# Preparing the recurrence inside the long convolution: paired low-rank products, key norms by Ln and Exp, key factors on ScalarE, keys on GpSimd

## The chip, the cores and the metric

One core of one Trainium2 chip runs the whole program in one launch. The metric is the device time of that launch in microseconds (us), lower is better; several executions are timed and their median is given. One more execution is taken with the hardware profiler, and every time in the sections on the trace is from it, counted from the start of its span.

## The reference

The model has two layers over 256 context tokens and 256 latent tokens of width 1024. Each layer is a feed-forward half step, a token mixer and a second feed-forward half step, each closed by a residual with LayerNorm. The mixer of the first layer, where the change lies, projects the tokens once and feeds two branches: a long convolution of order 2 (done by a discrete Fourier transform as matrix products), and a bidirectional RWKV-7 recurrence. What the recurrence needs is prepared like this:

```python
kk = heads(k * k_k)
kk = kk / jnp.maximum(jnp.sqrt(jnp.sum(kk * kk, -1, keepdims=True)), 1e-12)
for d, (wd, ad) in enumerate(((wdf, adf), (wdb, adb))):
    w_log = -jax.nn.softplus(-(w0[d] + jnp.tanh(wd) @ w_up[d]).astype(f32)) - 0.5
    decay = jnp.exp(-jnp.exp(w_log))
    a = jax.nn.sigmoid((a0[d] + ad @ a_up[d]).astype(f32))
    kd = k.astype(f32) * (1 + (a - 1) * k_a)
...
y = x1 * bidir_long_conv(v, filt[:, 0, 0], filt[:, 0, 1], skip[0])
y = x2 * bidir_long_conv(y, filt[:, 1, 0], filt[:, 1, 1], skip[1])
...
bonus = jnp.sum(r * k_sum * r_k, -1, keepdims=True) * v
```

`k_sum` is the sum of `kd` over both directions. The scan itself uses `decay`, `kd`, `kk` and `kk * a`.

## The kernel before

All engines run their own program and meet at semaphores. Activations lie with the 1024 channels on the partitions, eight tiles of 128x512 (512 tokens: 256 of context, 256 latent). The feed-forward parts and the projections are fp32 products split in three rounded products (`mm3`); their weights stream in by SyncE's DMAs, ScalarE makes the high part of each 128x1024 piece and GpSimd the remainder (`remainder`, L2137). The second layer's mixer is a gated linear attention, whose scans on VectorE are L2041.

In the first layer's mixer TensorE first makes 27 tiles of the projection `z`; ScalarE (L759) and VectorE (L1789, L1792) take each out of PSUM, and eight turned tiles (L1182, ScalarE L751) become `vtok` and `x1tok`. Four stages follow, in the order in which each engine's program is written:

1. The long convolution, two passes `o` over two segments `s`. TensorE makes the spectrum of each segment (`hy_f`, 8 products of 128x512 each), VectorE multiplies it with the filter (L1806 to L1814, twelve instructions for one segment, `hy_mul`), TensorE transforms back (`hy_i`), and VectorE multiplies with the gate (L1823 in the first pass, L1826 in the second, `hy_done`).
2. After `hy_done` has reached 4: sixteen low-rank products of 64 rows each (`lora_psum`, eight with `w_up` and eight with `a_up`), each taken by ScalarE as a Sigmoid (L773 for the decay rates `sgw`, L777 for `aa`). VectorE makes the raw keys `kk` (L1834), sums the rates along time in 32 scans of 128 tokens (L1843) and subtracts the middle of each chunk (L1853).
3. ScalarE squares `kk` (L781), TensorE sums the squares over the heads (`kk_sum`), ScalarE takes the root (L784). VectorE makes the key factors for both directions (L1866), the keys (L1869, L1872), the reciprocal of the norm (L1875, L1877), the normed keys (L1879) and the two products `aa` (L1883). GpSimd makes the bonus input meanwhile (L2176 to L2188) and clears two buffers and the first identities (L2190 to L2195). ScalarE copies the turned values (L788) and makes the first decays by Exp (L809).
4. TensorE sums the bonus over the heads, VectorE multiplies it into `zv` (L1888), clears the state (L1889), reports `prepared`, and fills the first four operand slots (`first_slots`, L1898 and L1899) beside GpSimd's (L2205). Then the recurrence begins with `strict(0)`: eight groups `gi`, each with seven levels of small products. L1310 and L968 are TensorE's helpers for transposes and products, so L968 is the line of nearly every product.

The tiles of the mixer are all slices of one SBUF tensor, `arena`, so the rows name `arena` for most operands.

## Time and profile before

| | us |
|---|---|
| three timed executions | 2390.08, 2400.35, 2410.40 |
| their median | 2400.35 |
| the profiled execution's own time | 2389.39 |
| its span | 2387.60 |
| outside the span | 1.79 |
| TensorE busy | 2186.0 (92%) |
| VectorE busy | 929.5 (39%) |
| ScalarE busy | 750.6 (31%) |
| GpSimd busy | 942.9 (39%) |
| mean granted TensorE clock | 0.955 |

The span runs from the first to the last instruction. The busy shares are means over the whole program; the stage that the change touches lies between about 634 and 770 us.

### The profile page before, as it was taken

The page shows a single profiled execution, that of the slowest core. Times are in us where ns is not written, and L with a number is a line of the kernel's source. Part 1 is how long each engine was busy: PE and PEld are TensorE (multiplying, and loading weights), DVE is VectorE, ACT ScalarE, POOL GpSimd, SP SyncE. Part 2 cuts the span into 40 slices and gives each one's busy share as a digit, 9 for nine tenths or more (in the row PEclk, how much of TensorE's full clock was granted, in tenths as well). Part 3 has the DMA queues.
Part 4 walks back from the last instruction along what each step waited for, and adds up shares of the span by engine and source line. Part 5 has one row for each costly group of instructions (what it writes and reads, how often), then busy time and mean ns, then how long its engine had stood idle before and what let it go on. Part 6 is the DMA issues. An engine that isn't in the chain of part 4 may idle for free.

```text
span 2387.6 us, 35611 instructions
## 1 busy us (share of the span) xinstructions
PE 2186.0 (92%) x15487; PEld 1764.1 (74%) x15487; DVE 929.5 (39%) x1354; ACT 750.6 (31%) x1097; POOL 942.9 (39%) x429
## 2 busy tenths in 40 slices
PE   5999999899982999997899999989999979988996
PEld 2677877678641888875677877767788858988996
DVE  3332123342369545545523132353213254447122
ACT  2422221353221222123612122262212246456343
POOL 0434434444106212104434443443444435537884
PEclk9999999999995989898999999999999989998998
DMA  9463354231000000003264345336332214314551
GB/s 325 158 218 144 106 177 167 71 120 65 9 0 0 3 2 3 7 31 130 81 202 154 102 156 206 115 97 204 131 106 75 85 44 147 107 38 140 184 189 52
DMA packets 176090, 259.66 MB, mean 109 GB/s; under 512 B 3925, under 2 KB 146275, under 8 KB 175876
## 3 DMA queue, kind: packets, MB, share of 16 engines
q1 hardware_dynamic: 173338, 252.65, 31.6%
q10 hardware_dynamic: 2602, 4.78, 0.6%
q8 instruction: 122, 2.00, 0.3%
q14 instruction: 28, 0.23, 0.0%
HBM read 256.37 MB, written 1.05 MB: 108 GB/s over the span
## 4 chain that ended last, share of the span: by engine, by line
PE 84%; DVE 8%; ACT 5%; issue 1%; DMA 1%; ACTq 0%; SPq 0%; POOL 0%; DVEq 0%; POOLq 0%
PE psum L968 83%; ACT arena L674 1%; ACT u_hi L679 1%; DVE h L1709 1%; DMA arena<-in_ada_w 1%; DVE arena L1866 1%; DVE arena L1877 1%; DMA arena<-in_x 1%; DVE tmp L1722 0%; ACT tmp L724 0%; ACTq L587 0%; DVE arena L1843 0%; PE psum L1310 0%; ACT L734 0%; DVE arena L2017 0%
## 5 line engine op out<-in xcount | busy, mean ns | idle before, releaser
L2137 POOL TENSOR_TENSOR w_lo<-arena,w_hi 128x1024 fp32r<-128x1024 f32 x332 | 817.3, 2467 | 1061.2 <-ACT w_hi L646 1058.9
L968 PE MATMUL psum<-u_hi,w_hi 128*128 128x512 f32 (+1 forms) x1888 | 699.4, 371 | 62.5 <-ACT u_hi L679 38.7
L968 PE MATMUL psum<-u_hi,w_lo 128*128 128x512 f32 (+1 forms) x1888 | 687.9, 364 | 0.0
L968 PE MATMUL psum<-u_lo,w_hi 128*128 128x512 f32 (+1 forms) x1888 | 668.3, 362 | 0.0
L646 ACT ACTIVATE w_hi<-arena 128x1024 fp32r<-128x1024 f32 x332 | 348.5, 1058 | 737.4 <-PE psum L968 725.4
L968 PEld LDWEIGHTS psum<-u_hi,w_hi 128*128 128x128 f32 x1888 | 361.9, 192 | 162.1 <-ACT u_hi L679 34.7
L968 PE MATMUL psum<-arena 64*64 64x64 f32 (+8 forms) x5892 | 380.1, 258 | 39.4 <-DVE arena L1899 18.4
L968 PEld LDWEIGHTS psum<-u_hi,w_lo 128*128 128x128 f32 x1888 | 362.5, 192 | 54.0
L968 PEld LDWEIGHTS psum<-u_lo,w_hi 128*128 128x128 f32 x1888 | 357.4, 190 | 52.8 <-issue 0.2
L968 PEld LDWEIGHTS psum<-arena 64*64 64x64 f32 (+5 forms) x5892 | 294.7, 150 | 117.7 <-issue 70.8
L1679 DVE TENSOR_TENSOR tmp<-psum,tmp 128x512 f32<-128x512 f32 (+1 forms) x88 | 54.9, 624 | 592.9 <-ACT tmp L698 592.9
L968 PE MATMUL psum<-hid_hi,w_hi 128*128 128x512 f32 (+1 forms) x704 | 257.4, 366 | 1.7 <-POOL w_lo L2137 1.1
L968 PE MATMUL psum<-hid_hi,w_lo 128*128 128x512 f32 (+1 forms) x704 | 255.3, 363 | 0.0
L968 PE MATMUL psum<-hid_lo,w_hi 128*128 128x512 f32 (+1 forms) x704 | 255.2, 363 | 0.0
L1683 DVE TENSOR_TENSOR hid_lo<-tmp,hid_hi 128x512 f32 (+1 forms) x88 | 198.6, 2257 | 10.8
L968 PEld LDWEIGHTS psum<-hid_hi,w_hi 128*128 128x128 f32 x704 | 132.9, 189 | 24.3 <-DVE mods L1617 1.7
L968 PEld LDWEIGHTS psum<-hid_lo,w_hi 128*128 128x128 f32 x704 | 132.9, 189 | 21.2 <-issue 0.7
L968 PEld LDWEIGHTS psum<-hid_hi,w_lo 128*128 128x128 f32 x704 | 132.9, 189 | 20.7
L698 ACT ACTIVATE tmp<-psum 128x512 f32<-128x512 f32 (+1 forms) x88 | 47.9, 545 | 303.2 <-PE psum L968 303.2
L823 ACT ACTIVATE arena<-psum 128x256 f32<-128x256 f32 x96 | 35.8, 386 | 206.0 <-PE psum L968 203.8
L1693 DVE SCALAR_TENSOR_TENSOR h<-psum,mods,h 128x256 f32<-128x256 f32 x56 | 22.3, 476 | 197.6 <-PE psum L968 197.6
L1709 DVE SCALAR_TENSOR_TENSOR h<-psum,mods,h 128x256 f32<-128x256 f32 x80 | 35.2, 478 | 147.3 <-PE psum L968 147.3
(244 smaller groups left out, 1599.0 us busy)
## 6 DMA issues: line engine op xcount, KB each, us to landing
arena<-in_ada_w SPq DMA_DIRECT2D x48, 1536.0 KB, 7.1
arena<-in_ffn_wg SPq DMA_DIRECT2D x44, 1024.0 KB, 5.5
arena<-in_ffn_wu SPq DMA_DIRECT2D x44, 1024.0 KB, 8.1
arena<-in_ffn_wd SPq DMA_DIRECT2D x20, 2048.0 KB, 8.7
arena<-in_ev_w_in SPq DMA_DIRECT2D x6, 2048.0 KB, 7.8
arena<-in_od_w_in SPq DMA_DIRECT2D x6, 2048.0 KB, 8.0
arena<-in_ffn_wd SPq DMA_DIRECT2D x4, 1024.0 KB, 5.1
arena<-in_ev_w_out SPq DMA_DIRECT2D x2, 2048.0 KB, 10.2
```

The lines of the kernel that those rows point to most:

```text
L646: act.activation(piece_shape(split_hi(pc), src), src, ACT.Copy).then_inc(S("hi_done"), 1)
L674: ins = act.activation(us[:, k, s_], hs[:, k, s_], ACT.Identity, scale=modv[:, 24 * (g % 3) + 8 + k, s_:s_ + 1], bias=modv[:, 24 * (g % 3) ...
L679: act.activation(uhv[:, k, T0:NT], uv[:, k, T0:NT], ACT.Copy).then_inc(S("u_hi"), 1)
L698: act.activation(tmp[:, jf * NT:jf * NT + TN], bank[2 * jf][:, 0:TN], ACT.Silu)\
L823: act.activation(blocks(zs[:, d].rearrange("p h t -> p (h t)"), m, d), blocks(bank[d], m, d), ACT.Copy).then_inc(S("zs"), 1)
L968: return pe.matmul(dst, w, x, start=first_, stop=last, skip_group_check=True)
L1679: ve.tensor_tensor(prod, bank[2 * jf + 1][:, 0:TN], prod, ALU.mult).then_inc(S("pairs_free"), 1)
L1683: ve.tensor_tensor(hid_lo[:, at], prod, hid_hi[:, at].bitcast(F32), ALU.subtract)\
L1709: ins = ve.scalar_tensor_tensor(out=hs[:, k, s], in0=bank[b][:, lo:lo + SEG], scalar=modv[:, 24 * (g % 3) + 16 + k, s:s + 1], in1=hs[:, k, s],
L1866: ve.tensor_scalar(dst, tile_of(aa[d], c), col("k_a", c), small[:, 20 + c:21 + c], ALU.mult, ALU.add).then_inc(S("ve_steps"), v.step())
L1877: ve.reciprocal(prep2, prep2).then_inc(S("ve_steps"), v.step())
L2137: pool.tensor_tensor(piece_shape(split_lo(pc), src), src, piece_shape(split_hi(pc).bitcast(F32), src), ALU.subtract).then_inc(S("lo_done"), 1)
```

## The change

The first pass of the convolution stays where it is. Into it and behind it, ahead of the second pass, goes the preparation:

- The squares of the keys are made by ScalarE straight from `zk` (`Square` with `k_k` as its scale) before the last `z` tile, and the four sums over the heads are TensorE's first products after the turned tiles. VectorE takes them with a floor of 1e-24, and ScalarE makes the reciprocal root by Ln and Exp with scale -0.5. Normed keys are then one VectorE instruction for each tile.
- The low-rank products go in eight pairs: one product on rows 0 to 63, one on rows 64 to 127, into the banks (2, 3) and (6, 7) by turns. The first pair stands before the back transform of the second segment, the other seven behind it.
- VectorE's order becomes: first pass, normed keys, scans, spectrum products of the second pass, the subtraction (now L1914), and then the outputs of the convolution (L1875) between the two `rates` products (L1882).
- The key factors are eight `Identity` activations on ScalarE with scale `k_a` and bias `1 - k_a`. The keys are two products on GpSimd; their sum, and the product with `zr`, are the bonus input; the factor `r_k` is now an activation on ScalarE.
- The values are turned into the banks that the low-rank products leave (`SPARE`), the first two ahead of the second back transform. One memset of GpSimd waits for the end of that transform.

The diff, cut to its core (the functions `multiplied`, `spectrum`, `back` and `back_turned` hold the same instructions as the loops before):

```diff
-prep = arena[:, 0:2048]
-prep2 = arena[:, 2048:4096]
-bonus = arena[:, 4096:6144]
+a_first = arena[:, 2048:4096]
+kk_rs = arena[:, 12288:14336]
+bonus = arena[:, 18432:20480]
+neg_kk, one_ka = small[:, 28:32], small[:, 20:24]
+PAIRS = ((2, 3), (6, 7))
+SPARE = (2, 3, 6, 7)
...
+        if i == ZT - 1:
+            act.wait_ge(S("z_done"), 20)
+            for c in range(CT):
+                act.activation(sgw[0][:, c * NT:(c + 1) * NT], zk[:, c * NT:(c + 1) * NT], ACT.Square,
+                               scale=col("k_k", c)).then_inc(S("kk_sq"), 1)
         act.wait_ge(S("z_psum"), i + 1)
...
     act.activation(bigt[:, 24], bigt[:, 24], ACT.Tanh).then_inc(S("lora_in"), 1)
+    act.wait_ge(S("kk_max"), 4)
+    act.activation(kk_rs, kk_rs, ACT.Ln).then_inc(S("kk_norm"), 1)
+    act.wait_ge(S("kk_norm"), 1)
+    act.activation(kk_rs, kk_rs, ACT.Exp, scale=-0.5).then_inc(S("kk_norm"), 1)
     act.activation(bigt[:, 26], bigt[:, 26], ACT.Sigmoid).then_inc(S("lora_in"), 1)
-    act.wait_ge(S("hy_done"), 4)
-    for q in range(16):
-        act.wait_ge(S("lora_psum"), q + 1)
...
-    act.wait_ge(S("kk_raw"), 1)
-    act.activation(prep, kk, ACT.Square).then_inc(S("kk_sq"), 1)
...
-        act.activation(prep2[:, i * NT:(i + 1) * NT], bank[i], ACT.Sqrt).then_inc(S("kk_norm"), 1)
...
+    tile_of = lambda ap, c: ap[:, c * NT:(c + 1) * NT]
+    for n in range(8):
+        c = n % 4
+        if n == 4:
+            act.wait_ge(S("hy_y1"), 4)
+        for d in range(2):
+            dst = tile_of(sgw[d] if n < 4 else a_first if d == 0 else aa[1], c)
+            act.wait_ge(S("lora_psum"), 2 * n + d + 1)
+            act.activation(dst, bank[PAIRS[n % 2][d]], ACT.Sigmoid, bias=col("w0" if n < 4 else "a0", 4 * d + c))\
+               .then_inc(S("lora_out"), 1)
+    act.wait_ge(S("lora_out"), 16)
+    for d in range(2):
+        for c in range(CT):
+            act.activation(tile_of(bonus if d else kd[0], c), tile_of(aa[1] if d else a_first, c), ACT.Identity,
+                           scale=col("k_a", c), bias=one_ka[:, c:c + 1]).then_inc(S("kd_f"), 1)
+    def v_out(b):
         act.wait_ge(S("v_turned"), b + 1)
-        act.activation(vt[:, b], bank[4 + b], ACT.Copy).then_inc(S("vt"), 1)
+        act.activation(vt[:, b], bank[SPARE[b]], ACT.Copy).then_inc(S("vt"), 1)
+    v_out(0)
+    v_out(1)
     def decays_of(j, d, from_, to):
...
-    for d in range(2):
-        decays_of(0, d, 0, 5)
+    decays_of(0, 0, 0, 5)
+    v_out(2)
+    v_out(3)
+    act.wait_ge(S("hy_i"), 4)
+    decays_of(0, 1, 0, 5)
+    act.wait_ge(S("bonus_k"), 1)
+    for c in range(CT):
+        act.activation(tile_of(bonus, c), tile_of(bonus, c), ACT.Identity, scale=col("r_k", c))\
+           .then_inc(S("bonus_in"), 1)
...
+    pe.wait_ge(S("z_done"), 24)
+    for i in range(4):
+        if i == 2:
+            pe.wait_ge(S("vtok"), 8)
+        pe.wait_ge(S("kk_sq"), i + 1)
+        mm(bank[4 + i], blk[:, :], sgw[0][:, i * NT:(i + 1) * NT], True, True).then_inc(S("kk_sum"), 1)
+    def lora(n):
+        c = n % 4
+        if n == 0:
+            pe.wait_ge(S("lora_in"), 1)
+            pe.wait_ge(S("ld_lora"), 32)
+        if n >= 2:
+            pe.wait_ge(S("lora_out"), 2 * (n - 1))
+        for d in range(2):
+            rows = slice(64 * d, 64 * d + 64)
+            mm(bank[PAIRS[n % 2][d]], (w_up if n < 4 else a_up)[rows, c * P:(c + 1) * P],
+               bigt[rows, 24 if n < 4 else 25], True, True).then_inc(S("lora_psum"), 1)
...
+    spectrum(0, 0)
+    pe.wait_ge(S("kk_max"), 4)
+    spectrum(0, 1)
+    pe.wait_ge(S("hy_mul"), 1)
+    back(0)
+    lora(0)
+    pe.wait_ge(S("hy_mul"), 2)
+    back(1)
+    for n in range(1, 8):
+        lora(n)
+    pe.wait_ge(S("hy_y1"), 2)
+    pe.wait_ge(S("lora_out"), 14)
+    spectrum(1, 0)
+    pe.wait_ge(S("hy_y1"), 4)
-    pe.wait_ge(S("kk_sq"), 1)
+    spectrum(1, 1)
+    pe.wait_ge(S("hy_mul"), 3)
+    back_turned(0)
+    v_turn(0)
+    v_turn(1)
+    pe.wait_ge(S("hy_mul"), 4)
+    back_turned(1)
+    v_turn(2)
+    v_turn(3)
-        mm(bank[i], blk[:, :], prep[:, i * NT:(i + 1) * NT], True, True).then_inc(S("kk_sum"), 1)
...
-    pe.wait_ge(S("bonus_in"), 1)
-    pe.wait_ge(S("kk_norm"), 4)
...
-    pe.wait_ge(S("vt"), 4)
+        pe.wait_ge(S("vt"), i + 1)
+        pe.wait_ge(S("bonus_in"), i + 1)
+        mm(bank[SPARE[i]], blk[:, :], bonus[:, i * NT:(i + 1) * NT], True, True).then_inc(S("bonus_sum"), 1)
...
+    ve.tensor_scalar(one_ka, par[:, PAR["k_a"]:PAR["k_a"] + 4], -1.0, 1.0, ALU.mult, ALU.add)\
+        .then_inc(S("bonus_coef"), 1)
+    ve.tensor_scalar(neg_kk, par[:, PAR["k_k"]:PAR["k_k"] + 4], -1.0, None, ALU.mult).then_inc(S("bonus_coef"), 1)
...
+    tile_of = lambda ap, c: ap[:, c * NT:(c + 1) * NT]
+    for i in range(4):
+        ve.wait_ge(S("kk_sum"), i + 1)
+        ve.tensor_scalar(tile_of(kk_rs, i), bank[4 + i], 1e-24, None, ALU.max).then_inc(S("kk_max"), 1)
...
+    def hyena_out(s):
+        ve.wait_ge(S("hy_i"), 2 + s + 1)
...
+    def rates(d):
+        ve.wait_ge(S("kd_f"), 4 * (d + 1))
+        ve.scalar_tensor_tensor(out=aa[d], in0=aa[1] if d else a_first, scalar=-1.0, in1=kk, op0=ALU.mult,
+                                op1=ALU.mult).then_inc(S("ve_steps"), v.step())
+    ve.wait_ge(S("bonus_coef"), 2)
-        ve.tensor_scalar(tile_of(kk, c), tile_of(zk, c), col("k_k", c), None, ALU.mult).then_inc(S("ve_steps"), v.step())
...
+        ve.scalar_tensor_tensor(out=tile_of(kk, c), in0=tile_of(zk, c), scalar=neg_kk[:, c:c + 1],
+                                in1=tile_of(kk_rs, c), op0=ALU.mult, op1=ALU.mult).then_inc(S("kk_ready"), 1)
+    for c in range(CT):
+        for d in range(2):
+            ve.wait_ge(S("lora_out"), 2 * c + d + 1)
...
+    for s in range(2):
+        multiplied(1, s)
...
-    for d in range(2):
-        for c in range(CT):
-            dst = tile_of(kd[0] if d == 0 else kd1_factor, c)
-            ve.tensor_scalar(dst, tile_of(aa[d], c), col("k_a", c), small[:, 20 + c:21 + c],
-                             ALU.mult, ALU.add).then_inc(S("ve_steps"), v.step())
-    ve.wait_ge(S("ve_steps"), v.n)
-    ve.tensor_tensor(kd[0], kd[0], zk, ALU.mult).then_inc(S("ve_steps"), v.step())
-    ve.wait_ge(S("ve_steps"), v.n)
-    ve.wait_ge(S("bonus_k"), 1)
-    ve.tensor_tensor(zk, zk, kd1_factor, ALU.mult).then_inc(S("ve_steps"), v.step())
-    ve.wait_ge(S("kk_norm"), 4)
-    ve.tensor_scalar(prep2, prep2, 1e-12, None, ALU.max).then_inc(S("ve_steps"), v.step())
-    ve.wait_ge(S("ve_steps"), v.n)
-    ve.reciprocal(prep2, prep2).then_inc(S("ve_steps"), v.step())
-    ve.wait_ge(S("ve_steps"), v.n)
-    ve.scalar_tensor_tensor(out=kk, in0=kk, scalar=-1.0, in1=prep2, op0=ALU.mult, op1=ALU.mult)\
-        .then_inc(S("ve_steps"), v.step())
-    ve.wait_ge(S("ve_steps"), v.n)
-    for d in range(2):
-        ve.scalar_tensor_tensor(out=aa[d], in0=aa[d], scalar=-1.0, in1=kk, op0=ALU.mult, op1=ALU.mult)\
-            .then_inc(S("ve_steps"), v.step())
+    hyena_out(0)
+    ve.wait_ge(S("kk_ready"), 4)
+    rates(1)
+    hyena_out(1)
+    ve.wait_ge(S("hy_done"), 4)
+    rates(0)
     ve.wait_ge(S("v_turned"), 4)
     for c in range(CT):
...
+        ve.tensor_tensor(tile_of(zv, c), bank[SPARE[c]], tile_of(zv, c), ALU.mult).then_inc(S("ve_steps"), v.step())
...
-    pool.wait_ge(S("hy_done"), 4)
-    pool.wait_ge(S("lora_psum"), 16)
     p = Count()
-    pool.wait_ge(S("bonus_coef"), 1)
-    pool.wait_ge(S("lora_out"), 16)
-    pool.tensor_tensor(bonus, aa[0], aa[1], ALU.add).then_inc(S("pool_steps"), p.step())
+    pool.wait_ge(S("kd_f"), 4)
+    pool.tensor_tensor(kd[0], kd[0], zk, ALU.mult).then_inc(S("pool_steps"), p.step())
+    pool.wait_ge(S("kd_f"), 8)
+    pool.wait_ge(S("kk_ready"), 4)
     pool.wait_ge(S("pool_steps"), p.n)
-    tile_of = lambda ap, c: ap[:, c * NT:(c + 1) * NT]
-    for c in range(CT):
-        pool.tensor_scalar(tile_of(bonus, c), tile_of(bonus, c), col("k_a", c), small[:, 24 + c:25 + c],
-                           ALU.mult, ALU.add).then_inc(S("pool_steps"), p.step())
+    pool.tensor_tensor(zk, zk, bonus, ALU.mult).then_inc(S("pool_steps"), p.step())
     pool.wait_ge(S("pool_steps"), p.n)
-    pool.tensor_tensor(bonus, bonus, zk, ALU.mult).then_inc(S("bonus_k"), 1)
-    pool.wait_ge(S("bonus_k"), 1)
-    pool.tensor_tensor(bonus, bonus, zr, ALU.mult).then_inc(S("pool_steps"), p.step())
+    pool.tensor_tensor(bonus, kd[0], zk, ALU.add).then_inc(S("pool_steps"), p.step())
     pool.wait_ge(S("pool_steps"), p.n)
-    for c in range(CT):
-        ins = pool.tensor_scalar(tile_of(bonus, c), tile_of(bonus, c), col("r_k", c), None, ALU.mult)
-    ins.then_inc(S("bonus_in"), 1)
-    pool.memset(arena[:, 6144:10240], 0.0).then_inc(S("nm_zero"), 1)
+    pool.tensor_tensor(bonus, bonus, zr, ALU.mult).then_inc(S("bonus_k"), 1)
     pool.memset(arena[:, 12288:13312], 0.0).then_inc(S("nm_zero"), 1)
     def reset(gi):
...
+    pool.memset(arena[:, 6144:10240], 0.0).then_inc(S("nm_zero"), 1)
     pool.wait_ge(S("nm_zero"), 2)
     pool.sem_inc(S("zeroed"), 1)
     pool.wait_ge(S("prepared"), 1)
```

GpSimd's program from the last split piece of the projection on stood like this (L2176 to L2188 make the bonus input, L2190 and L2191 clear buffers, L2195 writes identities):

```order
L2176 TENSOR_TENSOR arena<-arena 128x2048 [waits lo_done,bonus_coef,lora_out,lora_psum,hy_done]
L2180 TENSOR_SCALAR arena<-arena,par,small 128x512 [waits pool_steps]
L2180 TENSOR_SCALAR arena<-arena,par,small 128x512 x3
L2183 TENSOR_TENSOR arena<-arena 128x2048 [waits pool_steps]
L2185 TENSOR_TENSOR arena<-arena 128x2048 [waits bonus_k]
L2188 TENSOR_SCALAR arena<-arena,par 128x512 [waits pool_steps]
L2188 TENSOR_SCALAR arena<-arena,par 128x512 x3
L2190 MEMSET arena 128x4096
```

and in the changed kernel the same place reads (L2210 and L2214 make the keys, L2216 their sum, L2218 the product with `zr`):

```order
L2210 TENSOR_TENSOR arena<-arena 128x2048 [waits lo_done,kd_f]
L2214 TENSOR_TENSOR arena<-arena 128x2048 [waits pool_steps,kk_ready,kd_f]
L2216 TENSOR_TENSOR arena<-arena 128x2048 [waits pool_steps]
L2218 TENSOR_TENSOR arena<-arena 128x2048 [waits pool_steps]
L2219 MEMSET arena 128x1024
```

The first of them no longer waits for `hy_done`, the end of the convolution, but for the key factors (`kd_f`). VectorE before went from the outputs of the second pass (L1826) over the raw keys to the scans:

```order
L1826 TENSOR_TENSOR arena<-psum,arena 128x2x256 [waits hy_i]
L1826 TENSOR_TENSOR arena<-psum,arena 128x2x256
L1834 TENSOR_SCALAR arena<-arena,par 128x512 [waits hy_done]
L1834 TENSOR_SCALAR arena<-arena,par 128x512 x3
L1843 SCALAR_TENSOR_TENSOR arena<-ones,arena 128x128 [waits ve_steps,lora_out]
L1843 SCALAR_TENSOR_TENSOR arena<-ones,arena 128x128 x3
```

Now the scans (L1902) stand ahead of the second pass's spectrum products (L1858 on):

```order
L1902 SCALAR_TENSOR_TENSOR arena<-ones,arena 128x128 [waits lora_out]
L1902 SCALAR_TENSOR_TENSOR arena<-ones,arena 128x128 x3
L1906 TENSOR_SCALAR small<-arena 128x16 [waits ve_steps]
L1906 TENSOR_SCALAR small<-arena 128x16
L1858 TENSOR_TENSOR arena<-psum,arena 128x512 [waits hy_mul,hy_f]
L1859 TENSOR_TENSOR arena<-psum,arena 128x512
L1861 TENSOR_TENSOR arena<-arena 128x512 [waits ve_steps]
```

So whatever holds up the scans holds up the second pass. At the end of the stage VectorE had the key factors, the keys and the norm ahead of the bonus:

```order
L1866 TENSOR_SCALAR arena<-arena,par,small 128x512 x7
L1869 TENSOR_TENSOR arena<-arena 128x2048 [waits ve_steps]
L1872 TENSOR_TENSOR arena<-arena 128x2048 [waits bonus_k,ve_steps]
L1875 TENSOR_SCALAR arena<-arena 128x2048 [waits kk_norm]
L1877 RECIPROCAL arena<-arena 128x2048 [waits ve_steps]
L1879 SCALAR_TENSOR_TENSOR arena<-arena 128x2048 [waits ve_steps]
L1883 SCALAR_TENSOR_TENSOR arena<-arena 128x2048 [waits ve_steps]
L1883 SCALAR_TENSOR_TENSOR arena<-arena 128x2048
L1888 TENSOR_TENSOR arena<-psum,arena 128x512 [waits bonus_sum,v_turned]
```

and has now, behind the last spectrum product:

```order
L1914 TENSOR_TENSOR arena<-arena,small 128x2048 [waits ve_steps]
L1914 TENSOR_TENSOR arena<-arena,small 128x2048
L1875 TENSOR_TENSOR arena<-psum,arena 128x2x256 [waits ve_steps,hy_i]
L1875 TENSOR_TENSOR arena<-psum,arena 128x2x256
L1882 SCALAR_TENSOR_TENSOR arena<-arena 128x2048 [waits kd_f,kk_ready]
L1875 TENSOR_TENSOR arena<-psum,arena 128x2x256 [waits hy_i]
L1875 TENSOR_TENSOR arena<-psum,arena 128x2x256
L1882 SCALAR_TENSOR_TENSOR arena<-arena 128x2048 [waits kd_f,hy_done]
L1926 TENSOR_TENSOR arena<-psum,arena 128x512 [waits bonus_sum,v_turned]
```

Five kinds of instruction have left this end (L1866 to L1879); the subtraction and the convolution's outputs have come in.

## Rows read from the trace of the kernel before

**Rows 1.** Chain of waits through the stage: start us, us, what.

```profile
716.28 13.70 DVE arena L1866 x8
...
740.33 12.96 DVE arena L1877
...
769.72 2.09 PE psum L968 x16
```

**Rows 2.** Busy time by stretch: length, PE, PEld, DVE, ACT, POOL, PEclk, DMA, GB/s.

```profile
660.00:700.00 40.00, 36.15 (x115) 21.42 (x115) 21.70 (x36) 0.00 (x0) 0.00 (x0) 1.00 0.00 1
723.00:751.00 28.00, 6.22 (x8) 2.53 (x8) 27.90 (x8) 2.45 (x7) 27.73 (x13) 0.51 0.00 0
...
832.00:853.00 21.00, 21.00 (x206) 19.31 (x208) 6.17 (x12) 2.79 (x8) 2.02 (x2) 0.51 0.00 1
907.00:927.00 20.00, 19.06 (x335) 16.37 (x336) 9.52 (x21) 2.99 (x9) 2.68 (x3) 1.00 0.01 3
```

**Rows 3.** Timeline of TensorE: start us, us, what, count [idle before, releaser].

```profile
636.07 14.00 PE L968 MATMUL psum<-arena 128*128 128x512 f32 x32 [2.00 <-DVE arena L1792]
...
690.23 7.17 PE L968 MATMUL psum<-tmp,arena 128*128 128x256 f32 x32 [1.09 <-DVE arena L1814]
...
744.78 6.55 PE L968 MATMUL psum<-arena,blk 128*128 128x512 f32 x8 [25.12 <-POOL arena L2188]
769.72 2.08 PE L968 MATMUL psum<-arena 64*128 64x128 f32 x16 [18.39 <-DVE arena L1899]
```

**Rows 4.** Timeline of VectorE through the stage.

```profile
643.24 0.69 DVE L1806 TENSOR_TENSOR arena<-psum,arena 128x512 f32<-128x512 f32 x1 [7.23 <-PE psum L968]
...
651.51 0.69 DVE L1806 TENSOR_TENSOR arena<-psum,arena 128x512 f32<-128x512 f32 x1
...
698.77 1.67 DVE L1834 TENSOR_SCALAR arena<-arena,par 128x512 f32<-128x512 f32 x4
700.73 10.20 DVE L1843 TENSOR_TENSOR_SCAN arena<-ones,arena 128x128 f32<-128x128 f32 x32 [0.29 <-ACT arena L773]
...
711.26 4.49 DVE L1853 TENSOR_TENSOR arena<-arena,small 128x2048 f32<-128x2048 f32 x2
```

**Rows 5.** Timeline of ScalarE in the stage.

```profile
705.39 4.77 ACT L777 ACTIVATE arena<-psum,par 128x512 f32<-128x512 f32 x8
...
718.45 2.06 ACT L788 ACTIVATE arena<-psum 128x512 f32<-128x512 f32 x4
```

**Rows 6.** Timeline of GpSimd: the bonus input.

```profile
716.52 4.58 POOL L2176 TENSOR_TENSOR arena<-arena 128x2048 f32<-128x2048 f32 x1 [102.92 <-DVE small L1860]
```

**Rows 7.** Timeline of VectorE at the first operand slots.

```profile
763.22 1.80 DVE L1898 TENSOR_TENSOR arena<-arena 128x512 f32<-128x512 f32 x1 [0.15 <-DVE arena L1889]
764.94 1.75 DVE L1899 TENSOR_TENSOR arena<-arena,rs 128x512 f32<-128x512 f32 x1
```

**Rows 8.** Timeline of GpSimd at the same place.

```profile
763.21 1.26 POOL L2205 TENSOR_TENSOR arena<-arena 128x512 f32<-128x512 f32 x1 [12.18 <-DVEq L1891]
764.43 1.71 POOL L2205 TENSOR_TENSOR arena<-arena,tmp 128x512 f32<-128x512 f32 x1
```

**Rows 9.** Timeline of VectorE in the second layer: scans of 512, one by one.

```profile
2018.77 1.20 DVE L2041 TENSOR_TENSOR_SCAN arena<-arena 128x512 f32<-128x512 f32 x1
...
2025.06 3.30 DVE L2041 TENSOR_TENSOR_SCAN arena<-arena 128x512 f32<-128x512 f32 x1
```

**Rows 10.** Timeline of GpSimd in the second layer, at the same place.

```profile
2023.50 7.05 POOL L2137 TENSOR_TENSOR w_lo<-arena,w_hi 128x1024 fp32r<-128x1024 f32 x2 [10.28 <-ACT w_hi L646]
2027.24 3.31 POOL L2137 TENSOR_TENSOR w_lo<-arena,w_hi 128x1024 fp32r<-128x1024 f32 x1
```

**Rows 11.** Chain of waits in the recurrence: start us, us, what.

```profile
831.25 28.18 PE psum L968 x336
...
907.40 2.45 PE psum L968 x32
...
911.26 15.97 PE psum L968 x288
```

153 lines of the change are left out of this document (56 added, 97 removed).

## The prediction

> **What bounds the kernel now.** I read the chain of waits first. TensorE holds it nearly everywhere, but between the end of the projection, 636.07, and the first product of the recurrence, 769.72, it runs through VectorE for long stretches: the key factors take 13.70 us, the reciprocal 12.96 us [rows 1, 3]. That stage lasts 133.65 us, 5.6% of the span, and only there does the change move work. The busy shares by stretch come next. During the convolution TensorE is busy 36.15 of 40 us, but VectorE only 21.70 and ScalarE and GpSimd not at all; after it VectorE is busy all the time (27.90 of 28 us) and TensorE is not (6.22) [rows 2]. The work behind the convolution could therefore lie in VectorE's gaps within it. The same view gives the granted TensorE clock: 1.00 (2.4 GHz) in the convolution, 0.51 behind it, where TensorE idles. The timelines of each engine then give the durations.
>
> **The unit prices.** A full product of 128x512 costs 14.00/16 = 0.875 us, a back transform 7.17 us [rows 3]. At the low clock the four bonus sums took 6.55 us, 1.64 each [rows 3]. VectorE's twelve instructions for one segment take 651.51 - 643.24 = 8.27 us; a scan of 128 takes 10.20/32 = 0.32 us; a two-input instruction over 2048 columns takes 4.49/2 = 2.25 us [rows 4]. ScalarE takes 4.77/8 = 0.60 us for a tile of 512 with a bias and 2.06/4 = 0.52 us for a plain copy [rows 5]. GpSimd takes 4.58 us for a product over 2048 [rows 6].
>
> **What happens where VectorE and GpSimd meet.** This decides the sum. At 763.21 GpSimd starts a product (1.26 us), at 763.22 VectorE starts one whose inputs both lie in SBUF. VectorE's ends at 765.02, 0.55 us after GpSimd's end. GpSimd's next, issued at 764.43, ends at 766.14, 1.12 us after VectorE's end; and VectorE's next ends 0.55 us after that one [rows 7, 8]. So each waits for the whole instruction of the other, one for one. Scans do it as well: in the second layer a scan that takes 1.20 us alone takes 3.30 us against GpSimd's remainders, and GpSimd's 3.31 us [rows 9, 10]. VectorE's products that read PSUM do not show it.
>
> **The change part by part.**
> 1. Squares and norms. ScalarE's squares (4 x 0.6 us) lie under the last projection tile, where it waits for TensorE. The four sums cost 4 x 0.875 = 3.5 us on TensorE; they begin at about 634.1, right behind the turned tiles, where it waited until 636.07. So the first spectrum begins 1.5 us later. VectorE's four floors (0.6 each), and Ln, Exp and their table loads on ScalarE, end by about 646, beside spectra: nothing.
> 2. First pass. Its length stays; it ended at 659.72 + 7.13 on TensorE and will end at 668.3. The first low-rank pair hides in a wait for VectorE.
> 3. After it VectorE does two gate products (1.3), four normed keys (4 x 0.6 = 2.4) and 32 scans (10.2): to 682.0 if nothing blocks. TensorE and ScalarE pass the seven pairs along meanwhile. If two products on different rows run together, a pair costs ScalarE's 2 x 0.6 = 1.2 us: 668.3 + 1.0 + 7 x 1.2 = 677.7. That they can is seen in the recurrence's first products: eight of 64 rows and 128 columns took 2.08 us at the low clock [rows 3], where eight full ones in a row would take 8 x 1.64/4 = 3.3 us. If they run one after the other, TensorE's 1.75 us decide: 668.3 + 12.3 = 680.6. I take 677. The eight key factors follow on ScalarE, 0.6 to 0.7 us each (a scale column more than the 0.60 measured): four by 680.3, all by 683.
>    The Trainium skill ("ScalarE: Activation LUTs", section "Rules for kernel authors") says to put multiplies and adds on VectorE, not ScalarE. The row bears the price out: VectorE alone does a tile in 1.67/4 = 0.42 us [rows 4]. By that rule the factors would be 3.3 us on VectorE against some 5 us on ScalarE; but they took 13.70 us on VectorE beside GpSimd [rows 1], and ScalarE is waiting here, so this sum has no term for them.
> 4. GpSimd. Its first key product starts at 680.4 with the fourth factor. Six scans are then left. Four GpSimd instructions of 4.4 to 4.6 us follow each other with gaps of 0.1 us, and by rows 7 to 10 each lets one VectorE instruction with two SBUF inputs through: here a scan of 0.32 us. So the last scans end at about 699.8, not 682.0. Without the blocking the second pass would wait for its spectrum until 677 + 7.0 = 684, so the blocking costs 16 us. From the other side it costs nothing if scans slip between. If the pairs are slow, GpSimd starts at about 684 and blocks the spectrum products instead, of which two in three read PSUM: less is lost, but all is later, and the end moves by about 1 us only.
> 5. Second pass. VectorE 700.2 + 2 x 8.27 = 716.8 (0.3 for GpSimd's identities in it). TensorE has both spectra by 691 and idles to 708.6, when the first half of the products is there. Before, 25 us of idling were followed by low-clock sums [rows 2, 3]. I take the low level for the first 6.5 us (the sums' length) and get 10.4 us for the back transform: 719.0. Two turned blocks (1.0) and the second back transform at the high clock (7.2): 727.2; two blocks more: 728.2.
> 6. VectorE: subtraction 4.5 (721.3), first output 1.3, first rate product 2.25 (724.9), wait for the transform, second output 1.3 (728.6), second rate product 2.3 (730.9). ScalarE: two copies of values to 728.8, five decays (2.0) to 730.8, then the four `r_k` activations. They are queued behind the decays, so the bonus sums start at 731.5 and end at 735.0; the product, the memset and `prepared` are at 735.3. GpSimd's late memset (3.5 us from 727.3) ends before that. The key sum was ready at 700.
> 7. From 763.2 to 769.72, 6.5 us, the first slots were filled; that stays: `strict(0)` at 741.9.
>
> The stage ends 769.72 - 741.9 = 27.8 us earlier, so 28. If the low clock is not granted in point 5, 31; if the whole transform runs at it (14.3), 24.  Nothing behind `strict(0)` changes.
>
> Against the profiled execution's own time (2389.39, of which 1.79 lie outside the span) that is 2361. But that execution is the fastest of four: with the three timed ones, 2390.08, 2400.35 and 2410.40, the middle is 2395.2, 5 us below the table's median. I take 2395.2 - 28 = **2367 us**.
>
> **The rivals.**
> - *The blocking doesn't happen* at this place: GpSimd and the scans run beside each other. Then the second pass starts at 684, TensorE never idles long, and the end comes at 718 to 723: 47 to 52 us saved, 2346 us. For it: in this stage scans of 128 never met GpSimd, whose first product starts at 716.52 [rows 4, 6]. Against: rows 7 to 10. The Trainium skill ("SBUF — State Buffer", "Who interferes with whom") also says that a VectorE instruction with two SBUF inputs and a GpSimd one that reads SBUF exclude each other for a whole instruction; by that rule this rival is out, and the trace agrees (3.30 against 1.20 us). Chance 0.12.
> - *The clock takes the rest of the stage too.* Idle from 691 to 708.6, TensorE stays low through both transforms (2 x 14.3), turns and sums (6.55): 708.6 + 14.3 + 2 + 14.3 + 2 = 741.2, then copies, decays, sums, the product and the slots, 1.1 + 2.0 + 0.6 + 6.6 + 1.1 + 6.5 = 17.9: 759. Saved 11: 2384 us. For it: 0.51 in the 28 us after the convolution, with little work on TensorE. Against: the two transforms are over 14 us of unbroken work even at the high clock, where the work that stayed low was 6.55 us long [rows 3]. Chance 0.11.
> - *The recurrence loses its clock* and the kernel gets slower. A piece of 336 products took 28.18 us at 0.51 (831.25 to 859.4), and the same piece 907.40 to 927.23 = 19.8 us at 1.00 [rows 2, 11]: 8.4 us for 20.5 us at the low level, 0.41 for each. The place of such a stretch is not set by the program's text, since both pieces hold the same products; that also fits the 20 us between the timed runs. Another start could add some. It decides from 28/0.41 = 68 us more at the low level on; with 100 more the kernel stands at 2395 + 13 = 2408 us. Against: a mean clock of 0.955 makes 2 x 0.045 x 2387.6 = 215 us at the low level in the whole span, and 68 would be a third more. Chance 0.04.
> - *The change doesn't interleave*: the pairs wait so long that the scans come no earlier. They need only the first pass, which ends at 668; I fold this into the slow-pair bound of point 3, 1 us.
>
> **How the numbers follow.** The forecast has 0.73, with a range of its own of 2356 to 2377 (24 to 32 us saved, and some 6 us between the middles of such runs). The low end of the whole range takes in the first rival, 2343; the high end the second, 2388. Faster by over 1% (under 2376), about what a measurement of this kernel can tell from no change: the first rival whole, 0.12, nearly four fifths of the forecast, 0.57, and nothing of the others: 0.69. Slower by over 1%: half of the third, 0.02. Within 1%: 0.29.
>
> **What would show it.** The first product of the recurrence at 742 (on the time scale of the trace before), not 718 or 759. GpSimd's four products from 680 to 699, each about 4.6 us, and four of the last six scans of VectorE stretched to 4.7 us each; spectrum products of the second pass from 700. TensorE idle from 691 to 708, its clock low at the start of the next transform. ScalarE's `r_k` activations behind its decays. If scans stay at 0.32 us beside GpSimd, step 4 is wrong; if the pairs end after 681, step 3; if the transforms take 14 us each, step 5. If the time behind the recurrence's first product, 2387.6 - 769.7 = 1617.9 us before, differs by more than 10 us, the clock there has moved the result, not the preparation.

## The result, and the profile after

The changed kernel takes 2369.23 us (median of 12 runs, 2357.89 to 2378.45); the kernel before, run beside it, 2389.80 us (median of 12, 2383.61 to 2410.40). The ratio is 0.9894, with a 95% interval of 0.9875 to 0.9914: 21 to 30 us saved, 25 in the middle. The medians themselves lie 20.6 us apart. 28 us and 2367 us were forecast. The profiled execution of the kernel after, the fastest of its 12, took 2357.89 us (span 2356.1, mean granted clock 0.960 against 0.955 before); its span is 31.5 us shorter.

The timeline of TensorE, kernel after (columns as in [rows 3]). Line numbers have moved: products are now L989.

```profile
633.52 3.60 PE L989 MATMUL psum<-arena,blk 128*128 128x512 f32 x8
636.96 13.90 PE L989 MATMUL psum<-arena 128*128 128x512 f32 x32
...
659.31 1.13 PE L989 MATMUL psum<-arena 64*128 64x512 f32 x4
660.52 7.13 PE L989 MATMUL psum<-arena,tmp 128*128 128x512 f32 x16
667.58 1.99 PE L989 MATMUL psum<-arena 64*128 64x512 f32 x8
670.06 2.29 PE L989 MATMUL psum<-arena 64*128 64x512 f32 x8 [0.49 <-ACT arena L789]
672.53 3.61 PE L989 MATMUL psum<-arena 64*128 64x512 f32 x12 [0.19 <-ACT arena L789]
676.32 13.97 PE L989 MATMUL psum<-arena 128*128 128x512 f32 x32 [0.18 <-ACT arena L789]
706.69 9.86 PE L989 MATMUL psum<-tmp,arena 128*128 128x256 f32 x32 [16.40 <-DVE arena L1866]
716.38 1.04 PE L1229 MATMUL psum<-ident,arena 128*128 128x128 f32 x8
717.26 7.07 PE L989 MATMUL psum<-tmp,arena 128*128 128x256 f32 x32
724.17 1.04 PE L1229 MATMUL psum<-ident,arena 128*128 128x128 f32 x8
728.38 5.37 PE L989 MATMUL psum<-arena,blk 128*128 128x512 f32 x8 [3.18 <-ACT arena L836]
```

The first row is the sum of the squares (forecast from 634.1), the second the two spectra of the first pass, the third the first low-rank pair, the fourth the back transform of the second segment. Then come the remaining low-rank pairs, the second pass's spectra, a wait of 16.40 us for VectorE, and the second pass's two back transforms. The recurrence's first product, the row that [rows 3] end with, starts at 740.78 and was 769.72: 28.94 us earlier (27.8 forecast). Behind it lie 2356.1 - 740.8 = 1615.3 us, 1617.9 before. So nearly the whole difference of the two profiled spans comes from the preparation.

Where those 16.40 us come from is seen on VectorE, kernel after:

```profile
667.69 1.29 DVE L1890 TENSOR_TENSOR arena<-psum,arena 128x512 f32<-128x512 f32 x2 [6.03 <-PE psum L989]
668.89 2.73 DVE L1895 SCALAR_TENSOR_TENSOR arena<-arena,small 128x512 f32<-128x512 f32 x4
671.54 18.74 DVE L1902 TENSOR_TENSOR_SCAN arena<-ones,arena 128x128 f32<-128x128 f32 x32
690.32 4.37 DVE L1906 TENSOR_SCALAR small<-arena 128x16 f32<-128x16 f32 x2
694.61 0.68 DVE L1858 TENSOR_TENSOR arena<-psum,arena 128x512 f32<-128x512 f32 x1
...
695.92 3.78 DVE L1861 TENSOR_TENSOR arena<-arena 128x512 f32<-128x512 f32 x1
699.73 0.69 DVE L1863 TENSOR_TENSOR arena<-psum,arena 128x512 f32<-128x512 f32 x1
...
714.82 4.49 DVE L1914 TENSOR_TENSOR arena<-arena,small 128x2048 f32<-128x2048 f32 x2
```

and on GpSimd, kernel after:

```profile
680.47 4.63 POOL L2210 TENSOR_TENSOR arena<-arena 128x2048 f32<-128x2048 f32 x1 [67.26 <-ACT arena L794]
685.27 4.73 POOL L2214 TENSOR_TENSOR arena<-arena 128x2048 f32<-128x2048 f32 x1 [0.17 <-POOL arena L2210]
690.08 4.49 POOL L2216 TENSOR_TENSOR arena<-arena 128x2048 f32<-128x2048 f32 x1
694.65 4.50 POOL L2218 TENSOR_TENSOR arena<-arena 128x2048 f32<-128x2048 f32 x1
```

The 32 scans took 10.20 us before [rows 4] and take 18.74 us now. The trace's summary of the scans that lie between 680.6 and 690.4 (counts, then the least, median and longest time of one in ns) holds the two long ones:

```profile
L1902 DVE TENSOR_TENSOR_SCAN arena<-ones,arena x4: 392/2532/4680, 680.4 to 685.6; 128x128 f32<-128x128 f32 x4
```

One VectorE instruction waits through each of GpSimd's four products: a scan (4.68 us), another scan (4.66), the small gather of the sums' first and last columns (L1906, 4.29) and a spectrum product (3.78). Their ends, 685.4, 690.3, 694.6 and 699.7, follow the ends of GpSimd's products, 685.1, 690.0, 694.6 and 699.2, by up to half a microsecond. GpSimd's copies of the identities behind its products stretch one more VectorE instruction, the spectrum product at 701.05, from 0.69 to 1.49 us.

On ScalarE, kernel after: the sigmoids, the eight factors, and at the end the `r_k` activations.

```profile
668.74 8.70 ACT L789 ACTIVATE arena<-psum,par 128x512 f32<-128x512 f32 x14 [7.01 <-PE psum L989]
677.47 5.75 ACT L794 ACTIVATE arena<-arena,small,par 128x512 f32<-128x512 f32 x8
...
727.52 2.55 ACT L836 ACTIVATE arena<-arena,par 128x512 f32<-128x512 f32 x4
```

The busy time by stretch, kernel after (columns as in [rows 2]):

```profile
703.00:707.00 4.00, 0.31 (x1) 0.31 (x2) 3.79 (x7) 0.00 (x0) 0.00 (x0) 0.50 0.00 0
707.00:713.00 6.00, 6.00 (x17) 4.82 (x17) 5.79 (x10) 0.00 (x0) 0.00 (x0) 0.57 0.00 0
713.00:717.00 4.00, 4.00 (x23) 3.54 (x22) 3.96 (x4) 0.00 (x0) 0.00 (x0) 1.00 0.00 0
717.00:728.00 11.00, 8.20 (x44) 7.09 (x42) 9.38 (x8) 7.45 (x16) 3.52 (x1) 1.00 0.00 0
728.00:733.00 5.00, 4.62 (x7) 2.02 (x8) 1.45 (x3) 2.08 (x4) 0.00 (x0) 0.66 0.00 0
```

### The profile page after: what moved, and what is told of

Its sections match the earlier page's. It is cut to its first block, busy times and chain, and to the rows that moved or that the text cites. A ratio compares the mean times of both kernels' runs of the same rounds, so it can differ in the third digit from the quotient of the medians.

```text
span 2356.1 us, 35614 instructions
## 1 busy us (share of the span) xinstructions
PE 2182.1 (93%) x15487; PEld 1761.0 (75%) x15487; DVE 911.3 (39%) x1345; ACT 762.3 (32%) x1111; POOL 933.2 (40%) x422
## 4 chain that ended last, share of the span: by engine, by line
PE 85%; DVE 6%; ACT 5%; issue 2%; DMA 1%; ACTq 0%; SPq 0%; POOL 0%; DVEq 0%; POOLq 0%
PE psum L989 84%; ACT arena L677 1%; ACT u_hi L682 1%; DVE arena L1902 1%; DVE h L1753 1%; DMA arena<-in_ada_w 1%; DMA arena<-in_x 1%; DVE tmp L1766 0%; ACT tmp L727 0%; ACTq L590 0%; PE psum L1354 0%; ACT L737 0%; DVE arena L1861 0%; DVE arena L2055 0%; DVE h L1820 0%
## 5 line engine op out<-in xcount | busy, mean ns | idle before, releaser
L989 PE MATMUL psum<-u_hi,w_hi 128*128 128x512 f32 (+1 forms) x1888 | 699.7, 371 | 61.9 <-ACT u_hi L682 37.9
L989 PE MATMUL psum<-u_hi,w_lo 128*128 128x512 f32 (+1 forms) x1888 | 688.8, 365 | 0.0
L989 PE MATMUL psum<-u_lo,w_hi 128*128 128x512 f32 (+1 forms) x1888 | 668.4, 362 | 0.0
L989 PEld LDWEIGHTS psum<-u_hi,w_hi 128*128 128x128 f32 x1888 | 362.4, 192 | 161.0 <-ACT u_hi L682 33.6
L989 PEld LDWEIGHTS psum<-u_hi,w_lo 128*128 128x128 f32 x1888 | 362.8, 192 | 54.0
L989 PE MATMUL psum<-arena 64*64 64x64 f32 (+8 forms) x5892 | 377.7, 257 | 25.3 <-DVE arena L1937 7.0
L989 PEld LDWEIGHTS psum<-u_lo,w_hi 128*128 128x128 f32 x1888 | 357.3, 190 | 52.9 <-issue 0.2
L989 PEld LDWEIGHTS psum<-arena 64*64 64x64 f32 (+5 forms) x5892 | 291.0, 150 | 105.7 <-issue 59.4
L989 PE MATMUL psum<-hid_hi,w_hi 128*128 128x512 f32 (+1 forms) x704 | 257.4, 366 | 1.7 <-POOL w_lo L2175 1.2
L989 PE MATMUL psum<-hid_hi,w_lo 128*128 128x512 f32 (+1 forms) x704 | 255.3, 363 | 0.0
L989 PE MATMUL psum<-hid_lo,w_hi 128*128 128x512 f32 (+1 forms) x704 | 255.3, 363 | 0.0
L989 PEld LDWEIGHTS psum<-hid_hi,w_hi 128*128 128x128 f32 x704 | 132.9, 189 | 24.4 <-DVE mods L1661 1.7
L989 PEld LDWEIGHTS psum<-hid_lo,w_hi 128*128 128x128 f32 x704 | 132.9, 189 | 21.2 <-issue 0.7
L989 PEld LDWEIGHTS psum<-hid_hi,w_lo 128*128 128x128 f32 x704 | 132.9, 189 | 20.6
```

Source lines behind the costliest of these rows:

```text
L989: return pe.matmul(dst, w, x, start=first_, stop=last, skip_group_check=True)
```

## The experiments

Each is an edit of the changed kernel, run once with a profile; at the end the changed kernel and one edit were run six times each. They are judged by the length of the stage, from the sums of the squares to the recurrence's first product, since the start of the stage moves by up to 3.4 us from trace to trace: 633.52 to 740.78 = 107.26 us in the changed kernel. The time of the whole kernel in each run, which doesn't always follow the stage, stands in a table behind the single experiments.

**The four key products left out.** GpSimd only passes the signal on; the recurrence gets keys and a bonus input that were not made.

```diff
-                pool.tensor_tensor(kd[0], kd[0], zk, ALU.mult).then_inc(S("pool_steps"), p.step())
...
-                pool.tensor_tensor(bonus, bonus, zr, ALU.mult).then_inc(S("bonus_k"), 1)
+                pool.sem_inc(S("bonus_k"), 1)
```

> The changed kernel with GpSimd's four products over 2048 columns left out (the keys and the bonus input are not made; everything else stays). Reference: in the changed kernel's trace the second pass's spectrum products on VectorE start at 694.6 us and the recurrence's first product (L989, 64x128, x16) at 740.8. Blocking theory (each GpSimd product holds one VectorE instruction with two SBUF inputs for about 4.3 us): scans end at 681.7, the second pass starts with its spectrum at 683.4, TensorE idles only 1.3 us before the back transform, which takes 7.2 us and not 9.9, and the first product comes at 722 to 724, 17 to 19 us earlier. Rival 1 (the scans wait for the low-rank outputs, the blocking lies over that wait): scans still end near 690, the first product within 3 us of 740.8. Rival 2 (the loss is TensorE's clock): scans short, but the first product only 3 us earlier.

The stage took 634.81 to 725.23 = 90.42 us, 16.8 less (the kernel 2351.76 us). VectorE's timeline in this kernel:

```profile
672.83 10.20 DVE L1902 TENSOR_TENSOR_SCAN arena<-ones,arena 128x128 f32<-128x128 f32 x32
683.06 0.26 DVE L1906 TENSOR_SCALAR small<-arena 128x16 f32<-128x16 f32 x2
684.75 0.69 DVE L1858 TENSOR_TENSOR arena<-psum,arena 128x512 f32<-128x512 f32 x1 [1.43 <-PE psum L989]
...
686.07 1.09 DVE L1861 TENSOR_TENSOR arena<-arena 128x512 f32<-128x512 f32 x1
```

and TensorE's, with a back transform that follows a wait of only 1.78 us:

```profile
693.36 7.17 PE L989 MATMUL psum<-tmp,arena 128*128 128x256 f32 x32 [1.78 <-DVE arena L1866]
```

The two scans and the gather are back at their own length; the spectrum product (L1861) takes 1.09 us instead of 3.78, 0.4 over its own 0.69, beside GpSimd's copies of the identities. The transform is at the high clock throughout (1.00 from 690 to 701). Where the theory had 17 to 19 us, 16.8 were measured. Counted from the start of the stage, the first back transform begins 14.6 us earlier and is 2.7 us shorter by the clock; some 0.5 us are lost behind it. It is 14.6 us and not the 15.9 that the four stretched instructions had lost, mainly because the second pass now waits 1.43 us for its spectrum. So GpSimd's products, not the number of scans or anything in the convolution, make nearly all of the changed kernel's 16.40 us of idle TensorE. Since this run leaves work out, it does not say by itself whether the products cost VectorE time wherever they are made; the next one does.

**The same products on VectorE**, ahead of the second pass; nothing is left out, GpSimd waits for them.

```diff
+                ve.tensor_tensor(kd[0], kd[0], zk, ALU.mult).then_inc(S("ve_steps"), v.step())
...
+                ve.tensor_tensor(bonus, bonus, zr, ALU.mult).then_inc(S("bonus_k"), 1)
                 for s in range(2):
                     multiplied(1, s)
```

> The changed kernel with the four products moved from GpSimd to VectorE, between the scans and the second pass. Blocking theory: VectorE pays 4 x 2.25 = 9 us and is not blocked; the scans end at 681.7, the second pass starts at about 691 (694.6 in the changed kernel) and has no stretched instruction in it, its last spectrum product ends at 707.5 (714.9), and the recurrence's first product comes at 733 to 734 (740.8). Rival 1 (no blocking cost): 9 us later, about 750. Rival 2 (clock): TensorE idles 9 us instead of 16 before the back transform, so it is 9.9 us long or 7.2; between these the first product moves by 2.7 us only.

The stage took 633.37 to 733.89 = 100.52 us, 6.7 less. Four products of 2.28 us cost VectorE 9.1 us, where those on the other engine cost it 15.9; the difference, 6.8, is the 6.7 us of the stage. The engine that has more to do is done sooner. The whole kernel was not faster in this run, though (2364.64 us); the table below shows why.

**GpSimd held back until the scans are through.**

```diff
+                ve.wait_ge(S("ve_steps"), v.n)
+                ve.sem_inc(S("scanned"), 1)
...
+                pool.wait_ge(S("scanned"), 1)
```

> The changed kernel with GpSimd's four products held back until the scans are done, so that they lie beside the spectrum products of the second pass, of which two in three read PSUM. Blocking theory: scans end at 681.7, the pass starts at 683.4; four of its eight instructions with both inputs in SBUF wait some 2.5 to 4 us each; the first segment's products end at about 703 (706.7 in the changed kernel), the second's at 711.5 (714.9), the recurrence's first product at about 738 (740.8). Rival 1 (no blocking): first segment ends at 691.6, first product at 723. Rival 2 (PSUM products are blocked too): the first segment ends after 706.

633.34 to 737.02 = 103.68 us, 3.6 less. VectorE's timeline in this kernel shows which instructions wait:

```profile
684.60 2.46 DVE L1861 TENSOR_TENSOR arena<-arena 128x512 f32<-128x512 f32 x1
687.09 0.69 DVE L1863 TENSOR_TENSOR arena<-psum,arena 128x512 f32<-128x512 f32 x1
687.70 0.68 DVE L1864 TENSOR_TENSOR arena<-psum,arena 128x512 f32<-128x512 f32 x1
688.41 3.56 DVE L1866 TENSOR_TENSOR arena<-arena 128x512 f32<-128x512 f32 x1
```

Products that read PSUM run at 0.69 us beside GpSimd; those with both inputs in SBUF wait out its product. Against GpSimd a program of two PSUM products and one SBUF product gets three instructions through where the scans get one, so the same four products of GpSimd cost less. Each still lets just one SBUF product through. The first back transform begins 4.7 us earlier than in the changed kernel; about 0.7 us of that go in the first slots, where here GpSimd's product came first (730.51 against VectorE's 730.53) and VectorE's took 1.79 us, as in [rows 7, 8].

**The second product of a low-rank pair on the first's rows.** The backward direction's decays and gates then come from the forward direction's inputs.

```diff
-                        rows = slice(64 * d, 64 * d + 64)
+                        rows = slice(0, 64)
```

> The changed kernel with the second product of each low-rank pair reading the first's rows (0 to 63) instead of rows 64 to 127, so that the two can't run side by side (the backward direction then uses the forward one's inputs). If pairs run side by side now and serially then: a pair takes 1.75 us instead of 1.0, the seven pairs behind the second back transform end at about 680 instead of 676.2, and the second pass's first spectrum starts there. By the blocking theory the end hardly feels it: GpSimd's products then start at 684 and lie beside the spectrum products, and the recurrence's first product comes at 738 to 742 (740.8). Rival (the low-rank pairs set the end): 744.5. If the pairs don't run side by side now, nothing moves at all.

TensorE's timeline in this kernel; the third row holds the pairs and the second spectra:

```profile
662.51 1.98 PE L989 MATMUL psum<-arena 64*128 64x512 f32 x4
664.42 7.13 PE L989 MATMUL psum<-arena,tmp 128*128 128x512 f32 x16
671.49 26.21 PE L989 MATMUL psum<-arena 64*128 64x512 f32 x60
```

The first pair takes 1.98 us here and 1.13 us in the changed kernel: on different rows the two do run side by side. The stretch from the pairs to the end of the spectra grows from 22.7 us (667.58 to 690.29) to 26.2. Yet the stage is not longer but 3.6 us shorter, 636.73 to 740.40 = 103.67 us: GpSimd begins at 687.5, after the scans, and the first back transform begins 2.2 us earlier, counted from the start of the stage, as in the experiment before. The other 1.2 us are in that transform's length, 8.68 us instead of 9.86, which the edit does not explain. The pairs do what they should, and here it is worth nothing to the end.

**The `r_k` activations ahead of the decays on ScalarE.**

```diff
+                act.wait_ge(S("bonus_k"), 1)
+                for c in range(CT):
+                    act.activation(tile_of(bonus, c), tile_of(bonus, c), ACT.Identity, scale=col("r_k", c))\
+                       .then_inc(S("bonus_in"), 1)
                 v_out(0)
                 v_out(1)
```

> The changed kernel with the four r_k activations of ScalarE moved ahead of the copies of the values and of the decays (the bonus input is there from 699 us on). In the changed kernel the bonus sums start at 728.4, because ScalarE comes to these activations behind the second direction's decays. Theory (ScalarE's order sets the start of the sums): the first two sums start when TensorE has turned the last values, 725.2, the others when their banks are copied, at 726; they end at 728.7 instead of 733.7, and the recurrence's first product comes 4 to 5 us earlier, at about 736.5. Rival 1 (VectorE's second rate product, which ends at 728.0, is the bound): 1 us earlier only. Rival 2 (the low clock makes the sums long wherever they are): 2 us earlier.

633.34 to 736.23 = 102.89 us, 4.4 less (the kernel 2353.83 us). TensorE's timeline in this kernel:

```profile
723.72 1.04 PE L1229 MATMUL psum<-ident,arena 128*128 128x128 f32 x8
724.60 3.60 PE L989 MATMUL psum<-arena,blk 128*128 128x512 f32 x8
736.23 2.08 PE L989 MATMUL psum<-arena 64*128 64x128 f32 x16 [8.04 <-DVE arena L1937]
```

The sums need 3.60 us instead of 5.37: without the wait of 3.18 us ahead of them they keep the high clock (1.00 from 724 to 729). Both the queue and the clock are mended by one edit. VectorE's product with the sums now starts at 727.46, right behind its second rate product, which bounds the rest.

**The norms by root and reciprocal**, the one part undone.

```diff
-                act.activation(kk_rs, kk_rs, ACT.Exp, scale=-0.5).then_inc(S("kk_norm"), 1)
+                ve.reciprocal(kk_rs, kk_rs).then_inc(S("ve_steps"), v.step())
```

> The changed kernel with this part undone in place: the norm by Sqrt on ScalarE and a reciprocal over 2048 columns on VectorE (13 us) ahead of the normed keys, instead of Ln and Exp. Theory: VectorE has no room there, so the scans start at 684.5 instead of 671.5; GpSimd's products lie beside them and block one each; scans end at about 711, and the recurrence's first product comes at about 754, 13 us later. Rival (the reciprocal is taken up by VectorE's waits, and by the blocking that would fall there anyway): under 4 us later.

634.52 to 755.09 = 120.57 us, 13.3 more. VectorE's timeline in this kernel:

```profile
669.89 12.94 DVE L1891 RECIPROCAL arena<-arena 128x2048 f32<-128x2048 f32 x1
682.87 5.67 DVE L1895 SCALAR_TENSOR_TENSOR arena<-arena,small 128x512 f32<-128x512 f32 x4
```

The reciprocal stands in front of the scans at its full 12.94 us, and the normed keys (2.73 before) meet GpSimd. In the changed kernel Ln and Exp cost ScalarE 1.91 us each, and each a table load of 1.28 us, all under the first spectra. This part alone is nearly half of the 28.9 us by which the stage's end moved.

**The factors on VectorE**, behind the scans.

```diff
-                        act.activation(tile_of(bonus if d else kd[0], c), tile_of(aa[1] if d else a_first, c), ACT.Identity,
-                                       scale=col("k_a", c), bias=one_ka[:, c:c + 1]).then_inc(S("kd_f"), 1)
+                        ve.tensor_scalar(tile_of(bonus if d else kd[0], c), tile_of(aa[1] if d else a_first, c),
+                                         col("k_a", c), one_ka[:, c:c + 1], ALU.mult, ALU.add).then_inc(S("kd_f"), 1)
```

> The changed kernel with the eight key factors made by VectorE behind the scans, as tensor_scalar of 512 columns (0.42 us each alone), instead of ScalarE (5.75 us for the eight). Theory (ScalarE's time there is free, VectorE's is not): factors end later by 3.4 us of VectorE's work plus one blocking, GpSimd starts at 683.5 instead of 680.5, the second pass starts at about 699 instead of 694.6, and the recurrence's first product comes 3 to 5 us later, at about 745. Rival (the factors are on the way to GpSimd, and the faster engine makes the products start earlier): 2 us earlier, about 739.

633.31 to 740.83 = 107.52 us, 0.3 more; neither the 3 to 5 us of the theory nor the 2 us of the rival came. VectorE's timeline in this kernel:

```profile
671.32 10.20 DVE L1897 TENSOR_TENSOR_SCAN arena<-ones,arena 128x128 f32<-128x128 f32 x32
681.56 7.93 DVE L1903 TENSOR_SCALAR arena<-arena,par,small 128x512 f32<-128x512 f32 x8
...
690.90 3.72 DVE L1856 TENSOR_TENSOR arena<-arena 128x512 f32<-128x512 f32 x1
```

The eight take 7.93 us, one of them held by GpSimd's first product, against 5.75 us on ScalarE, and here they lie on the path. But GpSimd starts with them, at 683.55, so two scans and the gather are spared, and its last three products lie beside the second pass, of whose instructions only one in three is held. The one pays for the other. So ScalarE as the place of the factors brought the changed kernel nothing by itself.

**Both mendings together**: the products on VectorE and the `r_k` activations ahead, run once with a profile.

> Both together: the four products on VectorE between the scans and the second pass, and the r_k activations ahead of the copies and decays on ScalarE. If both theories hold and don't share their gain, the recurrence's first product comes at 729 to 730 (740.8 in the changed kernel): 7 us from the products and 4 from the order. Rival (the end is set by one thing only, VectorE's chain): no more than the products alone give, 733 to 734.

633.49 to 730.07 = 96.58 us, 10.7 less, near the 6.7 + 4.4 of the two edits (2348.04 us).

The kernel's time follows the stage in only some of these runs:

| run | stage us | behind the first product us | mean clock, whole run | kernel us |
| --- | --- | --- | --- | --- |
| changed | 107.26 | 1615.3 | 0.960 | 2357.89 |
| products left out | 90.42 | 1624.8 | 0.958 | 2351.76 |
| products on VectorE | 100.52 | 1628.9 | 0.955 | 2364.64 |
| GpSimd behind the scans | 103.68 | 1625.1 | 0.955 | 2363.98 |
| pairs on the same rows | 103.67 | 1624.5 | 0.956 | 2366.73 |
| `r_k` ahead | 102.89 | 1615.8 | 0.960 | 2353.83 |
| root and reciprocal | 120.57 | 1614.9 | 0.957 | 2371.85 |
| factors on VectorE | 107.52 | 1611.4 | 0.962 | 2353.96 |
| both mendings | 96.58 | 1616.1 | 0.962 | 2348.04 |

Four runs lose 9 to 14 us behind the first product against the changed kernel, and most of it lies in the first 500 us there, which hold the recurrence. Here is that stretch in the changed kernel and then in the one with the products on VectorE (columns as in [rows 2]):

```profile
740.78:1240.78 500.00, 462.00 (x6546) 378.05 (x6547) 251.43 (x440) 141.30 (x268) 126.09 (x73) 0.92 0.20 64
```

```profile
733.89:1233.89 500.00, 463.39 (x6476) 381.41 (x6477) 247.33 (x437) 138.72 (x265) 121.09 (x71) 0.89 0.17 56
```

The granted clock there is 0.92 and 0.89. At two levels, 1.00 and half of it, that is 500 x 0.03 x 2 = 30 us more at the low one, some 12 us of time at 0.38 to 0.41 us for each. The other three have 0.90, and the runs that lose nothing 0.92 or 0.93. Neither the length of the stage nor the place of the first product sorts the two kinds. So a single run's kernel time, and each of these was run once, does not tell what an edit is worth; the stage does. The kernel with both mendings and the changed one were then run six times each on one chip.

> The changed kernel with both mendings (key products on VectorE, r_k activations ahead of the decays), timed in rounds beside the kernel before. Theory (the 10.7 us that the stage lost beside the changed kernel are lost to the end, since nothing behind the recurrence's first product depends on where it starts): 25 + 11 = 36 us below the kernel before, a ratio of 0.985, with the scatter of the medians 0.982 to 0.988. Rival (part of the gain is given back in the recurrence, by its clock): 0.988 to 0.990, as the changed kernel alone.

> The changed kernel as it is, timed in rounds on the same chip as the one above. Both theories: 0.988 to 0.991 of the kernel before, and about 11 us above the kernel with both mendings if the first theory holds, within 5 us of it if the rival does.

| kernel | runs | median us | ratio to before (95%) |
| --- | --- | --- | --- |
| before | 11 | 2390.18 | |
| changed | 6 | 2357.20 (2355.80 to 2368.31) | 0.9870 (0.9827 to 0.9914) |
| changed, both mendings | 6 | 2358.38 (2346.54 to 2360.05) | 0.9852 (0.9810 to 0.9895) |

TensorE's timeline in the traced one of the six runs of the kernel with both mendings:

```profile
701.04 9.49 PE L989 MATMUL psum<-tmp,arena 128*128 128x256 f32 x32 [9.75 <-DVE arena L1866]
...
730.65 2.08 PE L989 MATMUL psum<-arena 64*128 64x128 f32 x16 [8.03 <-DVE arena L1947]
```

The changed kernel's first product stands at 740.96 in its traced run; the stages are 96.1 and 107.3 us long. The ratios agree with the expectations within their intervals (0.985 for the mended one; the changed one came out a little better than expected), but they overlap, and the medians do not show the 11 us: they lie 1.2 us apart, and the other way round. By the mark that was set for this distance, within 5 us, that is the rival's result, while the ratio to the kernel before is the theory's. Each kernel's runs fall into groups some 12 us apart by the mean clock granted: the changed kernel took 2355.8 to 2358.2 us in four runs at 0.960 to 0.962 and 2368.2 to 2368.3 us in two at 0.955 to 0.956; the mended one 2346.5 to 2348.1 us in two at 0.961 to 0.962 and 2357.3 to 2360.1 us in four at 0.955 to 0.957. At like clock it is 8 to 10 us faster. That is near the 10.3 us between the two first products. Behind them the two traces, both of the group with the higher clock, are alike (1615.7 and 1615.3 us). Whether the mended kernel draws the lower clock more often because of the edits or by chance, six runs of each don't tell. So the stage's gain reaches the end where the clock is alike; that the mended kernel is faster in the median is not shown, and the rival, that some comes back through the clock, is not excluded.

## Why the prediction was right, and where its numbers were off

**What bounds the kernel** (the steps ahead of the parts). Right. The work behind the convolution moved into it, and the kernel gained what the stage lost: 28.9 us of 31.5 in the traces.

**Points 1 and 2**, squares, norms and first pass. The sums began at 633.52 (634.1 forecast) and took 3.60; the first pass ended at 667.7 (668.3). The whole time scale lies 0.6 us earlier, which is half of the 1.1 us by which the stage's end came ahead of the forecast; 0.4 of it was there before the stage, in its turned tiles (633.09 against 633.47).

**Point 3**, the pairs and the factors. The pairs ran side by side; the last sigmoid was done at 677.4 (677 taken), the factors took 0.72 us each, a little over the 0.6 to 0.7 taken: the fourth at 680.4, the last at 683.2. The scans began at 671.5, where the sum has 671.8. What the point says against VectorE as the place of the factors fell: the 13.70 us of [rows 1] had blocking in them, and the run with the factors there ended only 0.3 us later. The term missing from that comparison is how the start of GpSimd's products moves. The Trainium skill's rule of that point ("ScalarE: Activation LUTs", "Rules for kernel authors") holds for the price of a tile: 0.46 us for each of the seven that GpSimd did not hold, (7.93 - 4.73)/7, against 0.72 on ScalarE. Whether it pays at the end no run shows: the two places end 0.3 us apart. The bound for slow pairs, about 1 us later, was wrong: on the same rows the stage was 3.6 us shorter.

**Point 4**, the blocking. The size was right: (4.68 - 0.35) + (4.66 - 0.35) + (4.29 - 0.13) + (3.78 - 0.69) = 15.9 us for 16 forecast, and 16.8 us of stage with the products gone, 2.7 of which are the clock's. The mechanism, one VectorE instruction for each GpSimd instruction, was right as well. Two details were not. Four scans were left at GpSimd's start, not six; by the forecast's own numbers it was five, (682.0 - 680.4)/0.32, and the scans began 0.3 us earlier. Two of the four took 0.39 and 0.40 us: one that was just starting, and one at 685.31, between the two held ones, while GpSimd waited 0.17 us for its own first product. So only two of the four victims were scans, the others the gather and a spectrum product, and the scans ended at 690.3 instead of 699.8. That did not change the sum, since VectorE is in the path through all of it. GpSimd's copies of the identities cost 0.8 us in the second pass (1.49 - 0.69), where the forecast had 0.3. And the sentence that blocked spectrum products would lose less was right but small: with GpSimd behind the scans 3.6 us of the stage came back.

**Point 5**, second pass and clock. VectorE's second pass ended at 714.9 (716.8), the transform started at 706.7 (708.6). It took 9.86 us (10.4 forecast); the second one, 7.07, was at the high clock, as forecast. The mis-sized term is the length of the low level, 6.5 us taken from the sums in [rows 3], and some 5 measured: (9.86 - 7.17) x 2 = 5.4 us.

**Point 6**, the end on ScalarE and the bonus sums. The queue was named rightly: the sums waited 3.18 us for the first `r_k` activation. They began at 728.4, 3.1 us earlier than forecast, and took 5.37 us instead of 3.5, because behind that wait TensorE was at the low level again (0.66 in 728 to 733). The point left the clock out. `prepared` came at 735.0, 0.3 us before the sum's 735.3, by errors that cancel: 3.1 us early at the sums' start, 1.9 us more in them, 0.9 us more in the last product and the memset.

**Point 7**. The first slots cost 740.78 - 735.01 = 5.8 us against 6.5, since VectorE's first product was ahead of GpSimd's this time (0.69 us and 1.81 us, both from 735.16, where it had been 1.80 and 1.26 in [rows 7, 8]). The order is not the edit's: with GpSimd behind the scans it was the old one, and the slots cost 737.02 - 730.53 = 6.5 us.

**The base.** 2367 was 2395.2 - 28. The kernel before had its median at 2389.8 in these runs, 5.4 us lower, and the saving between the medians was 20.6 us, not 28. The two errors nearly cancel in the time (2369.2 against 2367); that it came so close is luck in part, for by the medians the saving lies under the 24 to 32 us that the forecast gave. The stage's 28.9 us are what two traces show; 25 (21 to 30) is what the runs show. A part of the difference can be read from the clock. The stage spent some 50 us at the low level before (0.90 in 690 to 723, 0.54 in 723 to 770) and some 25 after (0.65 in 690 to 707, 0.74 to 717, 0.83 to 741), so the mean of the whole kernel should have risen by about 0.005, as it did in the profiled runs (0.955 to 0.960). But over the 12 runs after, the middle one has 0.954. That is (0.960 - 0.954) x 2 x 2360 = 28 us more at the low level than in the profiled run, and at 0.38 to 0.41 us each some 11 us: 31.5 - 11 = 20.5, as the medians have it. Six later runs of the same kernel had 0.961 in the middle. What decides it wasn't found. No trace of a run near the middle of the 12 was kept; in the four experiments that lost time behind the first product, the additional low level lay mostly in the 500 us that hold the recurrence.

**The rivals.** No blocking: gone, by the stretched scans and by the run without the products; its time for that case, 718 to 723 for the first product, came near the 725.2 measured, 1.3 us of which are a later start of the stage. The low clock through both transforms: gone (0.57 for 6 us, then 1.00). The recurrence losing its clock: not seen in the traces of the two kernels, 1615.3 us behind the first product against 1617.9, but 9 to 14 us of it in four of the edited ones, and by the means of the clock some 11 us in the middle run. As a mechanism it is there; the 68 us more at the low level that would let it decide were not reached (28 by the estimate above). A change that doesn't interleave: gone.

## What to carry to other kernels

Moving a product from a busy VectorE to an idle GpSimd can cost VectorE more than the product itself: count one whole GpSimd instruction for every product moved, unless VectorE's work beside it reads PSUM (2.28 us each kept, about 4 us each moved, here). Look at what is queued ahead of a short operand chain on the engine that has nothing to do for the next 20 us; the `r_k` activations could have run from 699 on, and ran at 727.5. A wait of TensorE can cost more than itself, by the half clock of the work behind it (here behind a wait of 3.18 us, not behind one of 1.78 us). And where the clock moves the kernel's time by 10 us and more from run to run, judge an edit by the length of the stage in the trace, and check in repeated runs that it reaches the end.

## What the runs showed of the hardware

- Even a VectorE instruction of 128x16 elements that takes 0.13 us alone waits out a GpSimd product: 4.29 us. The number of instructions counts, not their size. It has one SBUF input and not two, as [rows 7 to 10] had; one of the eight factor instructions, of one tensor and two columns of scalars, was held as well (7.93 us for all). So the condition "two SBUF inputs", which the forecast took from those rows, is too narrow. The Trainium skill ("SBUF — State Buffer", "Who interferes with whom") names this operation, `tensor_scalar`, beside the two-input ones; the trace agrees that it is held, and does not show which mode it ran in.
- What the first work behind an idle stretch of TensorE paid did not grow with the stretch: the back transform of 7.17 us took 9.78 us after 9.75 us of idling, 9.86 after 16.40 and 9.43 after 30.14 (the run with the reciprocal). All traces with 9.7 us or more of idling lie between 8.68 us (same rows, after 9.98) and 10.07 (GpSimd behind the scans, after 11.73). After 1.78 us it took 7.17. But the bonus sums behind 3.18 us of idling took 5.37 us instead of 3.60, and 5.35 us even in the run without the products, where the clock was high through both transforms before.
- The time of the whole kernel follows its mean granted clock: 2357.89 us at 0.960 and 2378.45 us at 0.949 for the changed kernel. With 2 x (1 - clock) x span that is 188 and 242 us at the low level, so 0.38 us of time for each; 0.41 had been worked out from the recurrence's pieces [rows 2, 11].
